# A mixture-of-experts layer: gate-up weights reloaded in quarters instead of halves

## What is computed

```python
    comb = jax.nn.one_hot(g_top[:, 0], N_GROUPS, dtype=jnp.float32)[:, :, None] * w_group[:, None, :]
    out = jnp.zeros_like(t)
    for gi in range(N_GROUPS):
        gate, up = jnp.split(jnp.einsum('nd,edf->nef', t, w_gu[gi]), 2, axis=-1)
        hmid = jax.nn.silu(gate) * up * comb[:, gi, :, None].astype(t.dtype)
        out = out + jnp.einsum('nef,efd->nd', hmid, w_dn[gi])
    return out.reshape(*lead, D_MODEL)
```

## Time and profile before

| | |
|---|---|
| median of 3 runs | 508.91 us (504.84 to 508.98) |
| the profiled execution | 508.93 us |
| its span, first to last instruction | 506.8 us |
| mean granted clock of TensorE | 0.943 of full speed |
| TensorE busy with matmuls | 456.3 us, 90% of the span |
| VectorE, ScalarE busy | 194.2 us (38%), 101.9 us (20%) |
| DMA, SP's queue | 127.66 MB (10^6 bytes), 65.4% of 16 engines' span |
| gate-up loads of 1024 KB / of 512 KB | 60, median 15.8 us from issue to landing / 8, 17.4 us |
| down loads of 1024 KB / of 512 KB | 28, 17.2 us / 8, 15.9 us |

### The profile page before, as it was taken

The page is one execution under the profiler, slowest core; times in us unless marked ns, Lnnn a source line. Parts: engine busy times, 40 slices in busy tenths (PEclk is TensorE's granted clock), DMA queues, the critical chain, the costliest instruction groups (busy, mean ns, idle before and its releaser), DMA issues.

```text
span 506.8 us, 6958 instructions
## 1 busy us (share of the span) xinstructions
PE 456.3 (90%) x2699; PEld 254.2 (50%) x2699; DVE 194.2 (38%) x603; ACT 101.9 (20%) x248; POOL 18.0 (4%) x49
## 2 busy tenths in 40 slices
PE   5999999999999999999688999999996999779881
PEld 4556544555666756555474637554532535234220
DVE  1300001244553644636774235243450524314145
ACT  4021402253322313222200101001010102001023
POOL 6000021000000001000000000000000000000000
PEclk9799999999999989999769899699998999979987
DMA  8998652300008614004549999999999999999933
GB/s 297 347 387 234 214 205 75 133 1 0 0 1 311 249 43 126 25 1 167 207 145 378 400 373 422 415 360 420 412 422 412 420 416 416 422 411 416 408 154 124
DMA packets 38889, 131.36 MB, mean 259 GB/s; under 512 B 10482, under 2 KB 10534, under 8 KB 31176
## 3 DMA queue, kind: packets, MB, share of 16 engines
q1 hardware_dynamic: 37712, 127.66, 65.4%
q0 software_dynamic: 608, 1.62, 0.8%
q10 hardware_dynamic: 536, 1.62, 0.8%
HBM read 127.69 MB, written 3.19 MB: 258 GB/s over the span
## 4 chain that ended last, share of the span: by engine, by line
PE 75%; DMA 15%; DVE 4%; ACT 2%; issue 2%; SPq 1%; ACTq 0%; DVEq 0%
PE bank L1544 71%; DMA gu_ring<-in_w_expert_gate_up 14%; PE bank L1574 1%; PE bank L1664 1%; PE bank L1770 1%; SPq L533 1%; DMA X<-in_x 1%; ACT gu_ring L807 0%; DVE BT L1306 0%; DVE r_kT L1329 0%; DVE r_xT L1054 0%; PE bank L1740 0%; DVE BT L1303 0%; PE bank L1608 0%; ACT V L935 0%
## 5 line engine op out<-in xcount | busy, mean ns | idle before, releaser
L1544 PE MATMUL bank<-gu_ring,r_xT 128*32 128x512 f32 (+1 forms) x560 | 82.7, 629 | 11.7 <-DMA gu_ring<-in_w_expert_gate_up 11.7
L1544 PE MATMUL bank<-r_xT,gu_ring 128*128 128x384 f32 x192 | 66.2, 504 | 2.4 <-DVE r_xT L1054 2.4
L1544 PEld LDWEIGHTS bank<-gu_ring,r_xT 128*32 128x32 f32 (+1 forms) x560 | 26.2, 122 | 65.1 <-issue 64.4
L1544 PE MATMUL bank<-BT,r_qz 128*128 128x128 f32 x384 | 48.3, 289 | 4.5 <-DVE BT L1306 4.5
L1544 PEld LDWEIGHTS bank<-BT,r_qz 128*128 128x128 f32 x384 | 46.8, 204 | 9.9 <-issue 7.5
L1544 PEld LDWEIGHTS bank<-r_xT,gu_ring 128*128 128x128 f32 x192 | 37.5, 197 | 28.4 <-DMA gu_ring<-in_w_in 2.6
L1544 PE MATMUL bank<-r_xs 128*128 128x512 f32 x96 | 49.1, 643 | 0.0
L1544 PE MATMUL bank<-r_xT,dn_ring 128*128 128x384 f32 x128 | 42.6, 486 | 0.0
L1404 DVE TENSOR_TENSOR X<-X,bank 128x512 f32<-128x512 f32 x42 | 28.9, 688 | 21.8 <-PE bank L1544 21.4
L1544 PE MATMUL bank<-dn_ring,V 128*32 128x512 f32 x256 | 30.9, 619 | 5.8 <-ACT V L935 4.6
L1544 PEld LDWEIGHTS bank<-r_xT,dn_ring 128*128 128x128 f32 x128 | 24.0, 190 | 15.0
(11 more groups left out here) (315 smaller groups left out, 475.9 us busy)
## 6 DMA issues: line engine op xcount, KB each, us to landing
gu_ring<-in_w_expert_gate_up SPq DMA_DIRECT2D x60, 1024.0 KB, 15.8
dn_ring<-in_w_expert_down SPq DMA_DIRECT2D x28, 1024.0 KB, 17.2
gu_ring<-in_w_in SPq DMA_DIRECT2D x4, 2048.0 KB, 12.0
dn_ring<-in_w_in SPq DMA_DIRECT2D x2, 2048.0 KB, 19.2
gu_ring<-in_w_out SPq DMA_DIRECT2D x2, 2048.0 KB, 9.5
gu_ring<-in_w_expert_gate_up SPq DMA_DIRECT2D x8, 512.0 KB, 17.4
dn_ring<-in_w_expert_down SPq DMA_DIRECT2D x8, 512.0 KB, 15.9
r_xs<-in_cache_k SPq DMA_DIRECT2D x8, 256.0 KB, 6.4
```

The lines of the kernel that those rows point to most:

```text
L1544: return te.matmul(out, lhsT, rhs, start=start, stop=stop, **kw)
```

## The change

From step 1 on the gate-up weights are fetched in four quarters of the contraction (k = 0 and 1, 2 and 3, 4 and 5, 6 and 7) for four experts each. SP waits before each quarter until TensorE has multiplied the old one. For the ends of quarters 0 and 2 there is a new semaphore, `gu_quarter`, to which TensorE adds one after k = 1 and after k = 5; the ends of quarters 1 and 3 are signalled by `gu_mid` and `gu_full`, as before. The two quarters of a half count on the same semaphore, so that the counts for which TensorE waits become 32 a step instead of 16; step 0 is still loaded in halves. The places in which TensorE waits are the same. Down loads, and step 7's third and fourth quarter as such, stay as they were, but the third is released by `gu_quarter`. In steps 1 to 7 the gate-up loads become 112 (all of 512 KB) where there were 52 of 1024 KB and 8 of 512 KB.

```diff
@@ -586,19 +587,18 @@
             for n in range(1, QUADS):
-                sp.wait_ge(gu_mid, n)
-                for h in range(WIDE):
-                    load_up(n, h, 0)
+                for quarter, done, count in ((0, gu_quarter, 2 * n - 1), (1, gu_mid, n), (2, gu_quarter, 2 * n)):
+                    sp.wait_ge(done, count)
+                    for h in range(WIDE):
+                        load_up_quarter(n, h, quarter, ld_gu[quarter // 2][h])
                 sp.wait_ge(gu_full, n)
                 if n < QUADS - 1:
                     for h in range(WIDE):
-                        load_up(n, h, 1)
+                        load_up_quarter(n, h, 3, ld_gu[1][h])
                     sp.wait_ge(y_full, n)
                     for h in range(WIDE):
                         load_down(n, h)
                 else:
-                    for h in range(WIDE):
-                        load_up_quarter(n, h, 2, ld_gu[1][h])
                     for h in range(WIDE):
                         load_up_quarter(n, h, 3, ld_end)
@@ -1828,20 +1828,22 @@
                     for h in range(WIDE if n < QUADS - 1 or half == 0 else 0):
-                        pe.wait_ge(ld_gu[half][h], n * 16 + 16)
+                        pe.wait_ge(ld_gu[half][h], n * 32 + 16)
                     if n == QUADS - 1 and half == 1:
 
                         pe.wait_ge(c_evac, 2 * TT * n)
                         for i in range(4):
                             kept_rows(i)
                         for h in range(WIDE):
-                            pe.wait_ge(ld_gu[1][h], n * 16 + 16)
+                            pe.wait_ge(ld_gu[1][h], n * 32)
                     for k in range(half * HALF_K, (half + 1) * HALF_K):
                         if n == QUADS - 1 and k == KT - 2:
                             pe.wait_ge(ld_end, 16 * WIDE)
                         for h in range(WIDE):
                             rows = slice(h * SLOTS, (h + 1) * SLOTS)
                             ins = mm(bG[0][rows, :], xgT[n % 2][:, k, rows], gu_ring[:, h, k * 2 * F:(k + 1) * 2 * F], k == 0, k == KT - 1)
+                        if k in (1, 5):
+                            ins.then_inc(gu_quarter, 1)
                     ins.then_inc(gu_full if half else gu_mid, 1)
```

More of the change, by code:

```diff
@@ L373, in build @@
         gu_mid = sem("gu_mid")
+        gu_quarter = sem("gu_quarter")
         gu_full = sem("gu_full")
```

## The result

The changed kernel took 511.29 us (median of 22 runs, 506.31 to 514.17) against 508.43 us before (22 runs, 504.07 to 510.84): ratio **1.0058**, 95% interval 1.0036 to 1.0079. That is 2.9 us slower, with 1.8 to 4.0 as the interval. The forecast was 509.8, 0.9 us slower. So the direction and "within 1%" were right and the size was too small. The profiled execution has a span of 511.2 us, 4.4 more than that of before.

What follows compares the result with a forecast made beforehand. The DMA was taken to bound the expert loop from about 361 to 446.86 us, TensorE before and after. Earlier release -1.5, dearer short runs +2.4, the rest 0: +0.9 us on 508.91, giving 509.8 us, range 505 to 513.

Steps and rivals of the forecast that it cites:

- three stages: TensorE sets the pace to about 361 us, the DMA from there to 446.86, then TensorE again.
- Part (2): Gate-up loads of steps 3 to 6: quarters with 4 KB runs cost 0.6 us more per step, +2.4 us.
- upper bound of 1.32 for a quarter: Mean over the last 16 loads of 512 KB; at that price the dearer gate-up loads would cost 5.0 us.
- Part (1): Step 3's gate-up loads at 333 us: quarter 0 goes out earlier; gain 0.7 to 1.77 us, taken as 1.5.
- the late start: Step 3's loads issued only at 332.89 us; removing this alone gains at least 0.7 us of the 1.6 lost.
- Part (3): 52 more DMA issues on SP from step 1 on, 0.43 us each; cost 0 while the queue is full.
- Part (5): After 446.99 us, last step: quarter 3 lands at 478.2, needed at 478.3; price 0, uncovered 0.3 us.
- B: Faster: 4 KB runs in gate-up cost nothing and the dry spell closes; -1.6, 507.3 us; chance 0.20.
- C: Slower: a quarter costs 1.32 us or more; +5.0 - 1.5 and 0.3 to 1 in the tail, 513 us; chance 0.13.
- D: Quarter 0 comes no sooner or starts slowly, the dry spell stays, the price is paid; +2.4, 511.3 us; chance 0.12.
- the dry spell: DMA queue running low over 332 to 336 us before step 3's gate-up loads, a shortage of 1.8 us.

Runs made afterwards that it cites:

- Experiments 1, 4 and 5: 1: the change's quarter loads without the earlier release, 1.0054; 4: kernel before with down loads in 8 KB runs, 0.9962 and 0.9945; 5: the change plus those down loads, 1.0029.
- x4_first23: Kernel before with only the first half of steps 2 and 3 in quarters, released early by gu_quarter; 508.96 us, ratio 1.0007.
- x4_again: Second measurement of the kernel before with only the first half of steps 2 and 3 in quarters, released early; 508.81 us, ratio 1.0005.
- x1_late: The change's quarter loads, but both quarters of a half issued where the half was, without the earlier release, against the kernel before; 511.17 us, ratio 1.0054.
- experiment 4: Kernel before with down loads of steps 0 to 6 in runs of 8 KB instead of 4 KB; 506.69 us, 0.9962, and again 505.36 us, 0.9945.

## Why the prediction was right, and where it was off

**The bound.** Right: three stages, with the DMA setting the pace up to the last gate-up load of step 6 and TensorE after it. The page's chain of the changed kernel puts 13% on SP's issues and 8% on DMA, where it was 1% and 15%. Those issues stand in a queue that moves 407 to 414 GB/s, so they are the same bound under another name.

**Part (2), the price.** Right in kind and size. Quarters land 1.28 us apart, so a step's gate-up takes 20.48 us (20.4 in step 3), and a step from landing to landing 30.7 as forecast. Experiments 1, 4 and 5 agree with this being the whole of the loss, each within its interval: the price alone gives 1.0054, the change 1.0058, and longer runs elsewhere refund half. It is the run and not the size of the load, as the down loads of 1 MB show, which cost 2.56 us with runs of 4 KB. The upper bound of 1.32 for a quarter wasn't reached by the loads in the queue.

**Part (1), the gain from the earlier release.** This is the step that failed. What it said of the place was right. Quarter 0 of step 3 was issued in time, the windows from 332 to 336 us show 401 to 418 GB/s, and the queue came to 333 us no later than before: the last down load of step 2 lands 63.8 us after the loop's common zero, and 63.9 before. Step 3 then took 1.1 us less with loads that are 0.6 dearer, so 1.7 us of loss are gone from it, all that the prediction had counted there.

But they didn't last. Only 0.7 of them was the late start. The other 1.0 to 1.1 was the load that landed late at 349.3, and the changed kernel has such a load too, at 427.0. The prediction had this split in hand: 0.7 was its lower bound, and it named a slower DMA engine for the rest. It took 1.5. So in this pair of profiles the term is -0.7. The medians don't resolve 0.7 from nothing. x4_first23 and x4_again, which buy the release for 0.6 us or less, give 1.0007 and 1.0005 where 1.5 would have made 0.997 to 0.998; that is the lower end of both intervals. With a term of -0.7 to 0 the sum is +1.7 to +2.4 instead of +0.9, and 2.9 (1.8 to 4.0) was measured. That accounts for 0.8 to 1.5 of the 2.0 us by which the forecast was short; the remainder isn't placed.

**The sum in loop time.** -0.7 for the late start, 0 for the late load (1.1 us in the kernel before, 1.0 in the changed one), +2.4 for the price in steps 3 to 6 make +1.7; the loop measured +1.8.

**Part (3), SP's issues.** Right. SP stands longer in its issues, 12.67 us for the 16 of step 3, but before a full queue, and the down loads land in their place.

**Part (5), the tail.** I gave it 0, with a cover of 0.1 us, and 0.3 if that went. The second half of gate-up of step 7, in which quarter 3 is waited for, took 3.97 us instead of 3.64, so the cover was gone and there is a wait of 0.3. It cost nothing on the whole: counted from the last gate-up load of step 6, this half ends after 33.1 us where it was 33.3. This is that half and the last down multiplication, to set against the earlier trace rows:

```profile
479.18 3.97 PE L1544 MATMUL bank<-gu_ring,r_xT 128*32 128x512 f32 x32
...
493.43 1.92 PE L1544 MATMUL bank<-dn_ring,V 128*32 128x512 f32 x16
```

The 1.2 us by which the tail is longer lie behind it. From the end of that half to the last down multiplication it took 8.9 us before and 10.3 after, of the same work, the granted clock being 0.81 and 0.67 (the value before the DMA share; first row before, second row the change):

```profile
480.10:489.00 8.90, 5.98 (x24) 1.40 (x22) 4.37 (x10) 0.94 (x3) 0.00 (x0) 0.81 0.70 277
```

```profile
483.20:493.40 10.20, 7.30 (x22) 1.83 (x22) 4.38 (x10) 0.94 (x3) 0.00 (x0) 0.67 0.52 208
```

Near its start TensorE idles for the same 2.49 us in both. x1_late, as slow as the change in the medians, had a tail of 59.5 us, so I hold this for a difference of executions and not for a cost of the change; it isn't shown.

**The rivals.** B, the free short runs, is refuted by 1.28 and by experiment 4. C needed dearer quarters, which didn't come. D came out close in size, +2.4 and 511.3, but its reason is refuted: the dry spell was closed. A forecast by D's sum would have hit the median for a wrong reason.

## What to carry to other kernels

A transfer cut finer for an earlier release also shortens its contiguous runs. Every byte of the stage pays for that, while the release helps only at the queue's gaps. The additional issues cost nothing here, because the queue was full while SP stood in them. So look at the run length first: here the order of rows in a matrix that was loaded in 4 KB runs was free to choose, and a kernel with 8 KB runs there was 0.4 to 0.6% faster than the one before, though only part of that is traced to the runs. And before you count the whole loss around a gap in a saturated queue as gain, go through it load by load: only the late start was the gap's. A load that lands late for another reason can be there again later.

## What the runs showed of the hardware

- The price of 1 MB by contiguous run in a full queue: 2.56 us at 4 KB, 2.48 at 8 KB, 2.45 at 16 KB, independent of whether a load has 512 KB or 1 MB (at 4 KB).
- A load over 64 partitions runs at about half the rate (512 KB in 2.31 us against 1.28 over 128), even with loads for the other 64 behind it.
- In each of eleven profiles one load (in x4_again two) lands 0.7 to 1.6 us late between 340 and 430 us, 2.1 to 4.2 us after the start of an instruction-fetch packet of 1.0 to 1.1 us. In the five that ran dry between 329 and 334 us (down to 16 to 143 GB/s) it comes at 345 to 350 us; in the six with the earlier release it comes, or comes again, at 396 to 427 us. That the fetch causes it is not shown.
